# A three-stage transformer program on one core: the mLSTM's value projection with 512 moving columns instead of 256

## The reference, cut to what matters

```python
z = jnp.einsum("bsd,de->bse", h, w_in) + b_in          # h: 512 x 1024, w_in: 1024 x 3080
conv_a, conv_gate, q, k, v, o, i_pre, f_pre = jnp.split(z, ...)   # v: columns 2048 to 2560
...
s = jnp.einsum("bhtd,bhsd->bhts", qb, kb) * w_intra
num = jnp.einsum("bhts,bhsd->bhtd", s, vb) + w_inter * jnp.einsum("bhvk,bhtk->bhtv", C, qb)
```

## Time and profile before

| what | value |
| --- | --- |
| runs | 1653.36, 1653.97, 1655.54 us |
| median | 1653.97 us |
| profiled execution, first to last instruction (its own time) | 1651.3 us |
| TensorE busy | 1609.1 us, 97% |
| VectorE busy | 1268.9 us, 77% |
| ScalarE busy | 924.5 us, 56% |
| values on TensorE | 872.6 to about 914.3 us of the span |

### The profile page before, as it was taken

One profiled execution on the slowest core, in us unless ns is written; L12 is line 12 of the kernel. 1 busy time (PEld: TensorE's weight loads), 2 busy tenths in 40 slices (PEclk: granted clock), 3 DMA queues, 4 the chain that ended last, 5 costly groups with the idle time before them and its releaser, 6 DMA issues.

```text
span 1651.3 us, 20467 instructions
## 1 busy us (share of the span) xinstructions
PE 1609.1 (97%) x8362; PEld 1325.1 (80%) x8362; DVE 1268.9 (77%) x1455; ACT 924.5 (56%) x1078; POOL 258.2 (16%) x178
## 2 busy tenths in 40 slices
PE   6999999999999999999999999999999999999994
PEld 4668876668988989899888778888888888888883
DVE  6654877887568747475799975699999999999994
ACT  6433235543444435352533244688888878888884
POOL 0000021000047232310000100111221221221201
PEclk9999999999999999999999999999999999999997
DMA  8306822004222313231222101599999999999993
GB/s 342 128 1 253 301 94 77 0 0 155 76 102 77 137 68 128 77 128 52 103 77 78 44 34 64 210 419 386 371 371 383 382 357 369 372 373 364 385 366 119
DMA packets 55316, 322.92 MB, mean 196 GB/s; under 512 B 12736, under 2 KB 13760, under 8 KB 18610
## 3 DMA queue, kind: packets, MB, share of 16 engines
q1 hardware_dynamic: 43584, 307.91, 49.0%
q0 software_dynamic: 9504, 8.43, 2.3%
q10 hardware_dynamic: 2130, 5.22, 0.8%
HBM read 323.60 MB, written 23.07 MB: 210 GB/s over the span
## 4 chain that ended last, share of the span: by engine, by line
PE 93%; DVE 2%; DMA 2%; ACT 2%; issue 1%; POOL 0%; SPq 0%; ACTq 0%; DVEq 0%; POOLq 0%
PE ps L586 25%; PE ps L1488 21%; PE ps L1515 11%; PE ps L1101 7%; PE ps L776 5%; PE ps L1357 3%; PE ps L1024 2%; PE ps L752 2%; PE ps L1472 2%; PE ps L809 1%; DMA xT<-in_x 1%; PE ps L1497 1%; PE ps L888 1%; PE ps L1012 1%; ACT whi L1567 1%
## 5 line engine op out<-in xcount | busy, mean ns | idle before, releaser
L2244 DVE TENSOR_TENSOR wlo<-raw,whi 128x2048 fp32r<-128x2048 f32 (+1 forms) x256 | 583.4, 2300 | 123.5 <-ACT whi L1567 123.4
L1567 ACT ACTIVATE whi<-raw 128x2048 fp32r<-128x2048 f32 (+1 forms) x256 | 485.4, 1912 | 146.3 <-PE ps L1488 36.6
L1488 PE MATMUL ps<-whi,xH 128*128 128x512 f32 x512 | 202.7, 396 | 1.3 <-DVE xL L2353 1.3
L1488 PE MATMUL ps<-whi,xL 128*128 128x512 f32 x512 | 200.2, 391 | 0.0
L1488 PE MATMUL ps<-wlo,xH 128*128 128x512 f32 x512 | 199.3, 389 | 0.0
L586 PE MATMUL ps<-hH,whi 128*128 128x512 f32 x352 | 138.7, 394 | 0.3 <-ACT dmax L2050 0.3
L586 PE MATMUL ps<-hH,wlo 128*128 128x512 f32 x352 | 137.1, 390 | 0.0
L586 PE MATMUL ps<-hL,whi 128*128 128x512 f32 x352 | 137.0, 389 | 0.0
L3307 POOL DMA_INDIRECT sum_scratch<-yb,idt x30 | 48.8, 1625 | 422.5 <-ACT yb L2185 408.7
L1488 PEld LDWEIGHTS ps<-whi,xL 128*128 128x128 f32 x512 | 96.1, 188 | 20.8
L1488 PEld LDWEIGHTS ps<-whi,xH 128*128 128x128 f32 x512 | 96.1, 188 | 20.4 <-DVE xL L2353 1.5
(11 more groups left out here) (527 smaller groups left out, 3533.7 us busy)
## 6 DMA issues: line engine op xcount, KB each, us to landing
raw<-in_experts SPq DMA_DIRECT2D x192, 1024.0 KB, 7.7
raw<-in_streamed SPq DMA_DIRECT2D x92, 1024.0 KB, 4.8
xT<-in_x SPq DMA_DIRECT2D x1, 2048.0 KB, 17.1
sum_scratch<-xN ACTq DMA_DIRECT2D x2, 1024.0 KB, 9.1
Y<-sum_scratch SPq DMA_DIRECT2D x4, 512.0 KB, 5.0
out<-Y SPq DMA_DIRECT2D x4, 512.0 KB, 2.7
h_scratch<-hN SPq DMA_DIRECT2D x4, 384.0 KB, 2.6
ctxT<-in_ctx SPq DMA_DIRECT2D x1, 1024.0 KB, 18.4
```

The costliest lines, as they stand in the source:

```text
L1488: ins = e.matmul(b.t[:, :], l, w, start=(kk == 0 and i == 0), stop=(kk == 7 and i == 2))
L1567: e.activation(u.hi, u.raw, ACT.Copy).then_inc(*p.inc("hi", n, on="hi"))
L2244: e.tensor_tensor(u.lo, u.raw, u.hi.bitcast(F32), ALU.subtract).then_inc(*p.inc("lo", n, on="lo"))
```

## The change: units with half of the inputs and all outputs

The two units `U_V` now hold 512 of the 1024 inputs with all 512 outputs. `value(i, half)` multiplies one token tile with one unit: 4 k times 3 products of 512 moving columns into one bank. The call with `half` 0 takes and holds the bank, the one with `half` 1 goes on in it, adds the bias with one product of 512 columns and lets it go. ScalarE copies 128 x 512 once for a token tile, four times in all. So the first token tile needs both units before its bank is full.

```diff
@@ unit_table
-    wide("v", "w_in_2", 0, 8, 2048, 2560)
+    for half in range(2):
+        put("v", "w_in_2", 4 * half, 4 * half + 4, 2048, 2560)
@@ TensorE
-        def value(c, i):
-            u = units[U_V[c]]
-            b = ps.take(("vN", c, i), ("act", "vN", c, i))
-            p.wait_ge(*done("dma", "br"))
-            p.wait_ge(*done("dve", "lo", U_V[c]))
+        def value(i, half):
+            n = U_V[half]
+            u = units[n]
+            b = ps["vN", i] if half else ps.take(("vN", i), ("act", "vN", i), hold=True)
+            p.wait_ge(*done("dve", "lo", n))
             p.wait_ge(*done(*b.before))
-            prs = []
-            for k in range(8):
-                prs += tri((hH[:, k, i * 128:(i + 1) * 128], hL[:, k, i * 128:(i + 1) * 128]), (u.hi[:, k, :], u.lo[:, k, :]))
-            mm(e, b.t[:, 0:256], prs + [(one1[0:1, :], brow[0:1, c * 256:(c + 1) * 256])], p.inc("vN", c, i))
-            if i == 3:
-                p.also("use", U_V[c])
+            for k in range(4):
+                kk, sl = 4 * half + k, slice(i * 128, (i + 1) * 128)
+                for j, (l, w) in enumerate(tri((hH[:, kk, sl], hL[:, kk, sl]), (u.hi[:, k, :], u.lo[:, k, :]))):
+                    ins = e.matmul(b.t[:, :], l, w, start=(kk == 0 and j == 0), stop=False)
+            if half:
+                p.wait_ge(*done("dma", "br"))
+                ins = e.matmul(b.t[:, :], one1[0:1, :], brow, start=False, stop=True)
+                ins.then_inc(*p.inc("vN", i))
+                ps.drop(b)
+                if i == 3:
+                    p.also("use", n)
+            elif i == 3:
+                ins.then_inc(*p.inc("use", n))
@@ TensorE, written-out order
         value(0, 0)
         value(0, 1)
         weights(0)
-        value(0, 2)
+        value(1, 0)
         keys(0)
-        value(0, 3)
+        value(1, 1)
         weights(1)
-        value(1, 0)
+        value(2, 0)
         keys(1)
-        value(1, 1)
+        value(3, 0)
         weights(2)
-        value(1, 2)
+        value(2, 1)
         keys(2)
-        value(1, 3)
+        value(3, 1)
         weights(3)
@@ ScalarE: value copies 128 x 512; order
         use(U_V[0])
-        value(0, 0)
-        value(0, 1)
-        value(0, 2)
+        value(0)
         weights(0)
...
@@ VectorE, order
         weights(1)
-        use(U_V[1])
         queries(1)
         convolve(4)
         weights(2)
         convolve(6)
+        use(U_V[1])
         queries(2)
         convolve(6)
-        use(U_O[0])
         weights(3)
         convolve(4)
         queries(3)
         convolve(4)
+        use(U_O[0])
         states(0)
```

More of the change, by code:

```diff
@@ L1243, in states @@
             p.wait_ge(*done("act", "kw", h))
-            p.wait_ge(*done("act", "vN", 1, 3))
+            p.wait_ge(*done("act", "vN", 3))
             p.wait_ge(*done(*b.before))
@@ L1996, in act_program, with value @@
         p.stage("mlstm")
-        def value(c, i):
-            p.wait_ge(*done("pe", "vN", c, i))
-            copy(vN[:, i, c * 256:(c + 1) * 256], ps["vN", c, i].t[:, 0:256], p.inc("vN", c, i))
+        def value(i):
+            p.wait_ge(*done("pe", "vN", i))
+            copy(vN[:, i, :], ps["vN", i].t[:, :], p.inc("vN", i))
         def weights(h):
@@ L2023, in act_program @@
         use(U_V[0])
-        value(0, 0)
-        value(0, 1)
-        value(0, 2)
+        value(0)
         weights(0)
-        value(0, 3)
         keys(0)
-        use(U_V[1])
-        value(1, 0)
+        value(1)
         weights(1)
         keys(1)
-        value(1, 1)
-        value(1, 2)
+        use(U_V[1])
         weights(2)
+        value(2)
         keys(2)
-        value(1, 3)
         use(U_O[0])
+        value(3)
         weights(3)
```

## The result

The changed kernel takes 1669.02 us (median of 5 runs, 1664.78 to 1669.49), the kernel before beside it 1653.97 (5 runs, 1653.36 to 1655.54). The ratio is 1.0085, with an interval of 1.0074 to 1.0096. So it is slower, by 15.1 us where 6.2 were forecast, and the time lies 6.6 us above the range. The profiled execution has a span of 1667.2 us, 15.9 more than before, and a mean granted clock of 0.986 for 0.993. The two differences (15.1 and 15.9) don't agree because the profiled execution of before was one of the quick ones: here 1669.02 - 1667.2 = 1.8 us lie outside the span, and the 2.7 us that the prediction took for this hold 0.9 of scatter. The sum from the median was not touched by that.

The account below looks back on a forecast made before the run. TensorE, busy 97% of the span, was taken to bound the kernel. Idle +6.5, clock +1.6 and products -1.9 gave +6.2 us, so 1653.97 became 1660.2 us; the 8 in 10 range was 1657.6 to 1662.4.

Parts of the forecast that it names:

- Which way and where: At the first token tile's thirteenth value matmul, TensorE waits for `wlo58` until about 882.0: 6.5 us idle, so slower.
- Rival C: At the thirteenth matmul `wlo58` is already written by 875.45, so no wait, only savings: 1652.1 us, chance 0.05.
- The clock behind the stall: After TensorE's idle wait for `wlo58` its clock stays low for 3.0 to 3.8 us, losing 1.6 us.
- Rival A: At the wait for `wlo58` TensorE idles but its clock doesn't fall: +4.6, 1658.6 us, chance 0.07.
- The products: In the value products, wider matmuls and fewer biases and mode changes cost 27.04 us for 28.91: 1.9 us less.
- What the bias product costs: In the values, four bias products of 512 columns cost 1.17 us each with their mode changes, 4.68 us together.
- What is late next: After 882 us VectorE gets some 7 us of waits, but costs TensorE nothing more: 0, upper bound 2 us.
- rival B: At about 975 us TensorE waits for late VectorE results: +1 to +4 us more, about 1662.5 us, chance 0.07.
- Rival D: Further on, later waits take up part of the delay, at most 1.7 us: 1658.5 us, chance 0.03.

Follow-up runs that it names:

- the twin pair: Changed kernel with unit 58 split early and unit 60 split behind the taps, full float32 bias product with 128 rows or one: 1651.32 and 1656.86 us.

## Why the prediction was wrong

**Which way and where: right.** The kernel is slower; the wait stands at the thirteenth matmul, ends with `wlo58`, and nothing was moved that makes it. It cost 6.4 us for 6.5 forecast. Rival C, no wait, is refuted; the variant with the early split shows that its condition, `whi58` ahead of the sigmoids, was named rightly.

**The clock behind the stall: right.** It cost 1.8 us for 1.6. Rival A is refuted. The upper bound of 1.8 was too low: in the execution with unit 60 moved, the low clock behind the same stall cost about 3 us.

**The products: right in size.** 27.1 us for 27.04, a gain of 1.8 for 1.9, at the full clock. The pair with the fast bias says more: with the bias nearly free the wide products are 0.3 us ahead, so most of this gain was not the width of the products. It points to four bias products being cheaper than eight; that was not measured by itself.

**What the bias product costs: the step that failed.** The prediction priced four bias products of 512 columns by their columns and their changes of mode, 4.68 us, and had one term for the clock, +1.6 us behind the stall: it let the clock fall only where TensorE idles. In the profiled execution the clock fell four times more, for 6.7 us. Three of the four, 4.9 us, come just behind a one-row product with a four-row broadcast beside it; taking the product away, or giving it 128 rows at the same duration, takes these falls away in the profiled executions, and doubling it in the kernel before brings four. Before, the bias was cut in eight, each with 256 columns, and the clock held: 1.00 from 870 to 890, and in every window on to 950. Where the limit lies was not measured here, and the falls are not certain in each execution: in the profiled one of the variant with unit 60 moved they were missing, and the five executions of the changed kernel spread over 4.7 us, with mean clocks of 0.986 to 0.989.

The Trainium skill, page "TensorE: Matmul & The Clock Gate", section "Part 1: The HAM clock gate (the "warmup" mystery)", lets the clock depend on how busy TensorE was, and throttles after idleness. For the stall the trace agrees: 0.50 behind 6.4 us of idleness. For the falls at 890.5, 918 and 925 idleness is no account: TensorE was listed as busy without a gap, and the twin pair shows that the rows of a product matter too. The measurement decides.

**What is late next: wrong by one term.** The prediction took 0 with an upper bound of 2. VectorE's lateness indeed did not come back: it waits 13 us in all for `nm` and `wi`, where 7 were reckoned, and still has its wait of 2.3 us for the output gate at the end, as in the earlier trace rows. So rival B is refuted as it was put. Rival D is too: behind 990 us TensorE waits 1.3 and 0.5 us, as against 1.3 and 0.4 before, so nothing took up the delay. But `wlo60`, moved behind the last taps, now falls into the time in which GpSimd makes the diagonals, and TensorE waits 1.5 us longer for them. The prediction followed `wlo59` alone and never asked what runs on GpSimd at that moment.

**The fall at 941.6** is the one that stays open. It follows the wait for GpSimd in the changed kernel, and a fall at 932.5 does in the variant with the early split. But the kernels without the bias and with 128 rows have the same wait (3.4 and 2.9 us in total) and no fall, and the variant with the other order has the wait (2.9) and the one-row products and no fall there either. So its 1.8 us have no shown cause: neither the wait nor the one-row products bring it each time, and no run here separates them.

**The start**, +1.6 us in the profiled execution, is scatter between executions and no part of the change. The prediction allowed half a microsecond for the scatter of the median. For the kernel before that was enough (its medians on all chips lie within 0.3 us), but the changed kernel, with falls that come and go, scatters far more.

The forecast with the measured terms is 6.4 + 1.8 - 1.8 + 6.7 + 1.5 = 14.6 us, for 15.1 between the medians. The terms are read from one execution and set in afterwards: they say where the time went and are no second forecast.

## What to carry to other kernels

Price a matmul with one or a few rows in more than its columns: a long one-row product next to four-row ones can make TensorE lose half its clock for a few microseconds though it never idles, so give a bias 128 rows (a broadcast row against a matrix of 1/128) or put it into the reduced-precision mode, and look at the granted clock of every stretch and not at the busy share. An accumulation that crosses two weight units makes its first tile wait for both, so split the second one earlier. When an operation of VectorE is moved, ask what GpSimd is doing where it lands.

## What the runs showed of the hardware

- The granted clock fell to 0.50 for about 3.4 us each time while TensorE was listed as busy throughout, 1.6 to 1.8 us lost per fall. The rows of four products, 128 or one, make the difference between two kernels: 1651.32 and 1656.86 us, with mean clocks of 0.993 to 0.994 and 0.989 to 0.991.
- A 128 x 128 `tensor_scalar` of GpSimd took 0.60 us at its shortest; two took 1.7 to 1.9 us beside VectorE's taps and 3.17 us while VectorE ran a `tensor_tensor` of 128 x 2048.
- Behind the waits at the start of the program the clock stays low for a time that differs between executions: a mean of 0.86 or 0.72 from 28 to 40 us, 1.6 us in the span.
